# Differential attention, cross attention and merge as one program: moved norm and moved loads in a fused encoder layer

## What is computed

```
h = rmsnorm(x); proj = h @ w_in
o_a = gla_branch(...) * silu(z_a)
o_b = diff_attention(d_q, d_k, d_v) * silu(z_b)     # rmsnorm of each head's output
o_c = memory_cross_attention(c_q, mem) * silu(z_c)  # 256 memory tokens, 4 heads of 128
merged = sum_i sigmoid(gate_i) * (o_i @ w_branch_i)
y = rmsnorm(x + merged @ w_out)
```

## Time and profile before

| what | value |
|---|---|
| median of 3 runs | 3347.8 us (3347.14 to 3348.02) |
| span of the profiled execution | 3339.5 us |
| PE busy | 3254.0 us, 97% |
| DVE, ACT, POOL busy | 60%, 40%, 33% |
| diff ends, cross begins (PE) | about 2671 us |
| cross ends, merge begins (PE) | about 2778 us |

### The profile page before, as it was taken

One profiled execution on the slowest core, in us unless ns is written; L12 is line 12 of the kernel. 1 busy time (PEld: TensorE's weight loads), 2 busy tenths in 40 slices (PEclk: granted clock), 3 DMA queues, 4 the chain that ended last, 5 costly groups with the idle time before them and its releaser, 6 DMA issues. The chain is left out here.

```text
span 3339.5 us, 50988 instructions
## 1 busy us (share of the span) xinstructions
PE 3254.0 (97%) x19012; PEld 2544.6 (76%) x19012; DVE 2009.0 (60%) x4622; ACT 1331.0 (40%) x2171; POOL 1103.7 (33%) x511
## 2 busy tenths in 40 slices
PE   8999999999999999999999988999999898999998
PEld 6888888887888888888877865666666566888887
DVE  3322312226667666766667779888888567556654
ACT  3111111114334433444333336666766565223421
POOL 3322313244333333333333425555555442000000
PEclk9999999999999999999999989999999999999999
DMA  7545445465454544544459964122121268667562
GB/s 224 186 163 183 164 153 180 166 219 196 143 187 140 198 141 145 184 139 145 131 177 303 352 211 122 44 80 73 51 64 39 105 217 272 231 219 246 173 218 73
DMA packets 319014, 555.63 MB, mean 166 GB/s; under 512 B 35694, under 2 KB 115438, under 8 KB 318768
## 3 DMA queue, kind: packets, MB, share of 16 engines
q1 hardware_dynamic: 267296, 471.66, 43.4%
q10 hardware_dynamic: 51472, 80.71, 6.7%
HBM read 382.43 MB, written 169.82 MB: 165 GB/s over the span
## 5 line engine op out<-in xcount | busy, mean ns | idle before, releaser
L781 POOL TENSOR_TENSOR glaf_w_lo<-early_raw,glaf_w_hi 128x1024 fp32r<-128x1024 f32 x140 | 344.6, 2462 | 612.4 <-ACT glaf_w_hi L755 610.8
L810 PE MATMUL glaf_dense_acc<-h_hi,glaf_w_hi 128*128 128x512 f32 x1120 | 450.0, 402 | 0.5 <-ACT glaf_w_hi L755 0.5
L810 PE MATMUL glaf_dense_acc<-h_lo,glaf_w_hi 128*128 128x512 f32 x1120 | 438.4, 391 | 0.0
L810 PE MATMUL glaf_dense_acc<-h_hi,glaf_w_lo 128*128 128x512 f32 x1120 | 435.5, 390 | 0.0
L1814 DVE CUSTOM_DVE_ANT_0 front_p<-diff_s_ps,ahead_table 128x512 f32<-128x512 f32 x544 | 347.3, 687 | 70.7 <-PE diff_s_ps L1676 69.7
L555 POOL TENSOR_TENSOR proj_w_lo<-early_raw,proj_w_hi 128x1024 fp32r<-128x1024 f32 x84 | 202.8, 2414 | 477.3 <-DVE proj_w_hi L505 477.3
L1757 ACT ACTIVATE front_p<-front_p,diff_neg_max 128x2048 f32<-128x2048 f32 (+1 forms) x160 | 278.8, 1743 | 7.0 <-DVE diff_neg_max L1822 7.0
L1700 PE MATMUL diff_oT_ps<-diff_aT,diff_v 128*128 128x512 f32 x544 | 272.7, 602 | 4.8 <-ACT diff_aT L1751 4.8
L215 PE MATMUL proj_acc<-h_hi,proj_w_hi 128*128 128x512 f32 x672 | 262.9, 391 | 0.6 <-POOL proj_w_lo L555 0.6
L217 PE MATMUL proj_acc<-h_hi,proj_w_lo 128*128 128x512 f32 x672 | 261.6, 389 | 0.0
L216 PE MATMUL proj_acc<-h_lo,proj_w_hi 128*128 128x512 f32 x672 | 261.5, 389 | 0.0
(11 more groups left out here) (223 smaller groups left out, 7144.9 us busy)
## 6 DMA issues: line engine op xcount, KB each, us to landing
early_raw<-in_w_zg SPq DMA_DIRECT2D x180, 512.0 KB, 4.5
early_raw<-in_w_stream SPq DMA_DIRECT2D x80, 512.0 KB, 3.6
scratch_zg<-glaf_dense_out SPq DMA_DIRECT2D x140, 256.0 KB, 2.2
items_raw<-in_w_br SPq DMA_DIRECT2D x120, 256.0 KB, 3.0
merge_gate<-scratch_zg SPq DMA_DIRECT2D x120, 256.0 KB, 3.3
scratch_featT<-proj_out ACTq DMA_DIRECT2D x80, 256.0 KB, 2.4
items_br_hi<-scratch_item_hi SPq DMA_DIRECT2D x60, 256.0 KB, 5.9
items_br_lo<-scratch_item_lo SPq DMA_DIRECT2D x60, 256.0 KB, 6.6
```

The costliest lines, as they stand in the source:

```text
L781: pool.tensor_tensor(self.w_lo[:, s], self.raw[:, u % self.RAW], self.w_hi[:, s], ALU.subtract).then_inc(self.lo_split, 1)
L810: done = pe.matmul(self.acc[:, u % self.banks], a, x, start=i == 0, stop=i == self.PER - 1)
```

## The change

The three phases share one `Block`, so that no barrier stands between them; buffers that change hands are guarded by semaphore waits instead. diff's loops run to turn 82 on every engine (`OWN` = 83); the bodies of its turn loops become functions (`pe_turn`, `act_turn`, `dve_turn`, `pool_turn`), and cross calls them for turns 83 to 87 between its first tiles. On PE: scores 0, turn 83, scores 1, turn 84, scores 2, turn 85, scores 3, transposes 0, turn 86, scores 4. On ACT the evacuations of turn 84 alternate with the exponentials of tile 0; turn 85 precedes exponentials 1, turn 86 follows exponentials 4. On DVE turn 85 follows maximum 2, and turn 86 the evacuation of tile 0. On POOL turn 85 precedes the scaling of tile 1, and turn 87 that of tile 4.

Loads: memory 0 is asked for after turn 77 is mixed, q of chunks 0 and 1 after turn 78, z and memory 1 after turn 79. The stores of groups 18 and 19 are in cross's queue, behind the weight pieces and ahead of the item loads. At merge, weight pieces 4 to 6 come first, then the gates, both ahead of cross's last two chunks of stores; w_out and the gain stand between these two. The final clearing of semaphores follows the shared block. Some buffers are allocated in another order so that the overlaps fit. The preload of the Exp table in cross is gone.

```diff
@@ -74,6 +75,9 @@
                 used.clear()
                 self.nc.all_engine_barrier()
 
+        if shared is not None:
+            used.extend(self.allocated)
+            return shared
         self.ctx.callback(clear)
         return self.ctx.enter_context(self.nc.Block())
 
...
         LAST = TURNS + LAG + 1
+        OWN = LAST - 3
...
                             load_k(n)
             load_z(NG - 1)
-            sp.wait_ge(near_done, TURNS)
-            sp.wait_ge(far_done, TURNS)
-            front.load(sp)
-            for g in range(NG - 3, NG):
-                store(g)
-        @block.gpsimd
-        def _(pool):
-            pool.memset(ones[:, :], 1.0).then_inc(ones_ready, 1)
-
+
+            def combined(turns):
+                sp.wait_ge(near_done, turns)
+                sp.wait_ge(far_done, turns)
+
+            combined(TURNS - 2)
+            front.load_memory(sp, 0)
+            combined(TURNS - 1)
+            for c in range(2):
+                front.load_q(sp, c)
+            store(sp, NG - 3)
+            combined(TURNS)
+            for c in range(2):
+                front.load_z(sp, c)
+            front.load_memory(sp, 1)
+
...
             items.load_w(sp)
-            for semaphore, value in diff_stores:
+            diff.store(sp, diff.groups - 2)
+            diff.store(sp, diff.groups - 1)
+            for semaphore, value in diff.stores:
                 sp.wait_ge(semaphore, value)
             items.load(sp, 0, 2 * H)
             for c in range(2, NC):
                 sp.wait_ge(scores_done, TT * (c - 1))
                 front.load_q(sp, c)
                 if c >= 3:
-                    store(c - 3)
+                    store(sp, c - 3)
                     sp.wait_ge(gated, H * (c - 2))
                     front.load_z(sp, c - 1)
                 if c == 3:
                     sp.wait_ge(stored[0], 32 * H)
                     items.load(sp, 2 * H, 3 * H)
-            store(NC - 3)
+            store(sp, NC - 3)
             sp.wait_ge(gated, H * (NC - 2))
             front.load_z(sp, NC - 1)
-            store(NC - 2)
-            store(NC - 1)
 
...
@@ -1989,6 +2047,8 @@
                     pe.wait_ge(q_in[c % 2], 16 * (c // 2 + 1))
                 if n in (0, SEQS[0] // P):
                     pe.wait_ge(kT_in[sequence(n)], 16)
+                if n == 0:
+                    pe.wait_ge(diff.biased, diff.units_biased)
                 if n >= 2:
                     pe.wait_ge(p_ready, n - 1)
                 for h in range(H):
@@ -1997,6 +2057,8 @@
 
             def transposes(n):
                 pe.wait_ge(p_scaled, n + 1)
+                if n == 0:
+                    pe.wait_ge(diff.aT_ready, diff.units)
                 for k in range(MT):
                     if n:
                         pe.wait_ge((pT_dve, pT_act)[k], n)
@@ -2009,6 +2071,9 @@
                 pe.wait_ge(pT_dve, TT * (c + 1))
                 pe.wait_ge(pT_act, TT * (c + 1))
                 pe.wait_ge(v_in[sequence(c * TT)], 16)
+                if unit == 0:
+                    pe.wait_ge(diff.y_ready, diff.groups)
+                    pe.wait_ge(diff.outT_ready, diff.groups)
                 if unit >= 2:
                     pe.wait_ge(gated, unit - 1)
                 for k in range(MT):
@@ -2018,6 +2083,11 @@
             for n in range(N + BEHIND):
                 if n < N:
                     scores(n)
+                if n < LAG + 1:
+                    if n == LAG:
+                        transposes(0)
+                    diff.pe_turn(pe, CLOSE + n)
+                    continue
                 if 0 <= n - BEHIND < N:
                     values(n - BEHIND)
                 if 0 <= n - LAG < N:
@@ -2025,22 +2095,27 @@
 
         @block.scalar
         def _(act):
-            act.preload_act_table(ACT.Exp)
+            def exponential(n, h):
+                return act.activation(p[:, n % SLOTS, h], s_ps[:, n % 2, h], ACT.Exp, bias=neg_max[:, n % 2, h:h + 1], scale=SCALE,
+                                      accum_out=total[:, n % 2, h:h + 1])
 
             def exponentials(n):
                 act.wait_ge(max_steps, 2 * n + 2)
+                if n == 1:
+                    act.wait_ge(diff.values_done, diff.units)
                 if n >= 2:
                     act.wait_ge(inverted, n - 1)
                 if n >= SLOTS:
                     act.wait_ge(turned, 2 * (n - SLOTS) + 2)
                 for h in range(H):
-                    done = act.activation(p[:, n % SLOTS, h], s_ps[:, n % 2, h], ACT.Exp, bias=neg_max[:, n % 2, h:h + 1], scale=SCALE,
-                                          accum_out=total[:, n % 2, h:h + 1])
+                    done = exponential(n, h)
                 done.then_inc(p_ready, 1)
 
             def evacuate(n):
                 c, t = divmod(n, TT)
                 act.wait_ge(turned, 2 * n + 2)
+                if n == 0:
+                    act.wait_ge(diff.turned, diff.units)
                 if c >= 2 and t == 0:
                     act.wait_ge(values_done, H * (c - 1))
                 act.activation(pT[:, c % 2, 1, :, t * P:(t + 1) * P], t_ps[:, 1].rearrange("p (h t) -> p h t", h=H), ACT.Copy).then_inc(pT_act, 1)
@@ -2052,9 +2127,18 @@
                 act.wait_ge(gated, unit + 1)
                 act.activation(out_hi[:, c % 2, h], prod[:, unit % 2], ACT.Copy).then_inc(out_high, 1)
 
-            for n in range(N + BEHIND):
+            diff.act_turn(act, CLOSE)
+            act.wait_ge(max_steps, 2)
+            for h in range(H):
+                diff.evacuate(act, CLOSE + 1, h)
+                done = exponential(0, h)
+            done.then_inc(p_ready, 1)
+            diff.act_turn(act, CLOSE + 2)
+            for n in range(1, N + BEHIND):
                 if n < N:
                     exponentials(n)
+                if n == LAG + 1:
+                    diff.act_turn(act, CLOSE + 3)
                 if 0 <= n - LAG < N:
                     evacuate(n - LAG)
...
@@ -2101,6 +2187,8 @@
             for n in range(N + BEHIND + 1):
                 if n < N:
                     maximum(n)
+                if n == LAG - 1:
+                    diff.dve_turn(dve, CLOSE + 2)
                 if 0 <= n - 1 < N:
                     invert(n - 1)
                 if 0 <= n - BEHIND - 1 < N:
@@ -2109,16 +2197,23 @@
                     product(n - BEHIND)
                 if 0 <= n - LAG < N:
                     evacuate(n - LAG)
+                if n == LAG:
+                    diff.dve_turn(dve, CLOSE + 3)
                 if 0 <= n - N // 2 < items.SPLIT:
                     items.low(dve, n - N // 2)
 
         @block.gpsimd
         def _(pool):
+            diff.pool_turn(pool, CLOSE)
             for n in range(N):
+                if n == 1:
+                    diff.pool_turn(pool, CLOSE + 2)
+                if n == LAG + 1:
+                    diff.pool_turn(pool, CLOSE + 4)
                 pool.wait_ge(inverted, n + 1)
                 pool.tensor_tensor(p[:, n % SLOTS], p[:, n % SLOTS], inverse[:, n % 2].unsqueeze(2).broadcast_to([P, H, N_MEM]), ALU.mult).then_inc(p_scaled, 1)
 
-    return [(stored[b], 32 * H * ((NC + 1 - b) // 2)) for b in range(2)]
+        return CrossEnd(store, NC, scores_done, N, turned, 2 * N, values_done, gated, N, p_ready, [(stored[b], 32 * H * ((NC + 1 - b) // 2)) for b in range(2)])
 
...
@@ -2246,14 +2342,18 @@
                 sp.wait_ge(normed, n + 1)
                 sp.dma_start(rows(y, n * P, P), x[:, n % XS]).then_inc(y_out[n % XS], 16)
 
+            for u in range(AHEAD):
+                load_w(u + RAW)
+            sp.wait_ge(cross.scores_done, cross.tiles)
             for u in range(GS):
                 load_gate(u)
+            cross.store(sp, cross.chunks - 2)
+            sp.wait_ge(cross.turned, cross.turns)
             for kt in range(XS):
                 load_wo(kt)
             sp.dma_start(gain[:, :], final_gain).then_inc(gain_in, 16)
-            for u in range(AHEAD):
-                load_w(u + RAW)
-            for semaphore, value in cross_stores:
+            cross.store(sp, cross.chunks - 1)
+            for semaphore, value in cross.stores:
                 sp.wait_ge(semaphore, value)
             for c in range(NC):
...
@@ -2309,6 +2409,8 @@
 
             def wo_split(kt):
                 act.wait_ge(wo_in[kt % XS], 16 * (kt // XS + 1))
+                if kt == 0:
+                    act.wait_ge(cross.values_done, cross.units)
                 act.activation(wo_hi[:, kt], x[:, kt % XS], ACT.Copy).then_inc(wo_high, 1)
 
...
@@ -2344,6 +2446,8 @@
             def branch(u):
                 c, d, b = place(u)
                 s = u % RING
+                if u == 0:
+                    pe.wait_ge(cross.p_ready, cross.tiles)
                 pe.wait_ge(lo_split, u + 1)
                 if u >= RING:
                     pe.wait_ge(combined, u - RING + 1)
@@ -2356,6 +2460,7 @@
 
             def outputs(c):
                 if c == 0:
```

(11 more changed lines are left out.)

275 lines of the change are left out of this document (159 added, 116 removed).

## The result

The changed kernel takes 3349.5 us (median of 21 runs, 3346.4 to 3352.2), the kernel before, beside it, 3345.8 (median of 21, 3341.9 to 3348.0). The ratio is 1.0014, 95% interval 1.0007 to 1.0020: slower, by 3.7 us between the medians, by 4.7 by the ratio (2.3 to 6.7). 3339.6 was predicted, with a range of 3332 to 3345.5. The direction was wrong, the range too low.

The account below looks back on a forecast made before the run. TensorE, busy to the end, was taken to bound the kernel. Seam one's +1.65 and seam two's -9.8 sum to -8.15: span 3331.35, with 8.3 around it 3339.6 us; range 3332 to 3345.5.

Parts of the forecast that it names:

- The base: Span of the profiled execution, 3339.5 us, with 8.3 added at the end to reach the median of three runs, 3347.8.
- S0: Scores of cross tile 0, first in seam one's new order, taking the place of diff turn 83: start at 2646.4.
- S4: Scores of cross tile 4, seam one: start at 2669.85, 14.2 us sooner than 2684.10.
- the norm's chain: Last group's norm in seam one: VectorE done 2667.65, GpSimd's diagonal 2668.8, TensorE waits 0.8 us ahead of the spread.
- SyncE's queue: Seam one: q 2, behind group 19's store and 16 item loads, lands at 2696.7; a 14 us wait takes back the gain.
- S8: Scores of cross tile 8: start at 2696.8 instead of 2682.7; from there on +1.65 us with the low clock.
- rival (a): Both seams pay in full, with q 2 there by 2683: -24.0 us, 3323.8; chance 0.10.
- The low clock: After the wait at tile 8 its scores run at the lower clock: 1.74 us lost, as at tile 16.
- rival (c): Slower: after 14 us of idling before S8 the clock stays low; with 31 us more, 3354.6; chance 0.07.
- Seam two's gap: Cross to merge: merge follows the last values at once, 4.95 us and 0.15 of overlap, 5.1 won.
- Merge's first units: Start of merge: 1.5 us won from the cold start, 2.2 from unit 4's piece, 1.0 of 1.9 from other waits.
- Rival (b): Seam two pays only the seam; merge's 4.1 us of waits stay or come back elsewhere: -4.95, 3342.8; chance 0.15.

Follow-up runs that it names:

- e4: Changed kernel with q 2 loaded once tile 3's scores are done, ahead of group 19's store and the item loads: 3330.1 us, ratio 0.9959.
- e8: Changed kernel with stat allocated behind wo_lo, which begins at byte 117376 again: 3342.8 us, ratio 0.9993.
- e1: Changed kernel with stat 64 bytes wide instead of 32, so wo_lo begins at 117440: 3347.9 us, ratio 1.0006.
- e5: Changed kernel with SyncE's wait for cross's last stores moved to the first load that overwrites an item buffer: 3348.0 us, ratio 1.0010.
- e12: Kernel before with stat ahead of wo_hi (32 bytes off) and 96 bytes of padding ahead of wo_lo: 3346.4 us, ratio 1.0012.
- e2: Kernel before with stat (32 bytes) allocated ahead of wo_lo, nothing else: 3351.1 us, ratio 1.0022.
- e11: e9 plus q 4 loaded after tile 11's scores, and w_out's splits spread over merge units 4 to 18, loads two units later: 3318.5 us, ratio 0.9922.
- e9: Changed kernel with the edits of e4, e5 and e8, plus w_out's loads four units and ScalarE's splits two units later: 3325.2 us, ratio 0.9943.

## Why the prediction was wrong, point by point

**The base.** "8.3 around" the span was read wrongly: it is 1.8 (3352.2 against 3350.4), and the other 6.5 us were the distance of a quick execution to the median. In the sum this does no harm, since it only leads back to the median of three runs, 3347.8. But that median lay 2.0 above the one of 21 runs, 3345.8; from there the same sum gives 3337.7, so 2 us of the 3339.6 were luck.

**S0, S4, the norm's chain: right.** S0 was forecast at 2646.4 and S4 at 2669.85; less the 5.1 us by which the changed profile reaches the mark later, they came at 2646.4 and 2669.5, with the forecast wait of 0.8 at the spread.

**SyncE's queue: right.** The low half of group 19 was forecast for 2677.3 and items for 2680.3; less the drift its store was issued at 2678.5 and the first item at 2680.9; q 2 was issued at 2689.3, where the prediction had 2689.7. q 2 let S8 start 17.1 us after the first item, inside the 14.7 to 18.0, and S8 began at 2697.9 instead of 2696.8. That seam one would be won and given back at S8 is shown by the 13.62 us row and by e4. What rival (a) had over the forecast, 14 us at S8 and the low clock, is what e4 gave when the queue was turned round (13.8 and 3.1).

**The low clock: the term was too small.** 1.74 us was taken from tile 16, after 3.15 us of idling. After 13.62 us, S8 to S9 took 7.43 instead of 4.32 (2696.89 to 2701.21 before, S8 in the earlier trace rows): 3.1 us, since not only the scores but the values behind them ran slowly. Other versions with the same wait lost 3.1 (e8), 2.7 (e1) and 1.9 (e5). So the step's price was 3.1 where 1.74 stood; it and 1.1 us by which S8 came later make the first column's miss, less 0.3 from seam two. Nor is tile 16's price a fixed one: 0.1, 1.8 or 3.1 us after nearly the same idling (e12, before, e2). The clock recovered each time; rival (c)'s staying low didn't happen.

**Seam two's gap: right.** 5.1 us forecast; the values run into merge without idling, and the step from S9 to merge's first matmul is 5.4 us shorter (+4.16 against before at S9, -1.25 at merge, both from the mark).

**Merge's first units: this step failed.** 4.7 us were to be won (cold start, unit 4's piece, 1.0 of the others) and 0.85 were lost. Unit 4's wait did go. The sentence that failed is "q, z and stores go out ahead of them or wait for nobody": it looked at the pieces loaded early and not at the next one. The last stores now go out behind gates, w_out and the gain, while merge already runs; SyncE's wait for them, which had cost nothing, became 9.9 us, and weight piece 7 stood behind it. GpSimd has the same wait of its own ahead of w_out's low halves, which reuse memory that the stores still read. The two together are the step: SyncE's put off alone (e5) gave 0.3 us of the stage back, and with GpSimd's work spread as well (e11) 4.25 of the 5.55 missed. The prediction's "late next is VectorE", beside GpSimd, was the right engine; that the wait for the stores would bunch GpSimd's work, and so VectorE's stretching, was not seen. Rival (b) had this engine, but priced it as waits that stay, not as a new one with a clock drop behind it.

**The outputs: missing from the sum.** "Some buffers are allocated in another order so that the overlaps fit" stood in the description of the change and got neither a price nor a rival. It cost 6.2 us, and decides the sign of the result: without it (e8) the changed kernel isn't told apart from the one before. Even then the forecast gain of 8 didn't come; the other two misses took it.

The three misses, 2.2 + 5.55 + 6.2, are 13.95 us: forecast -8.15, came +5.8 by the marks of the two profiles. By medians it is +3.7 (interval 2.3 to 6.7).

## What to carry to other kernels

When barriers between phases fall, follow each queue past the seam up to its first wait for a landing, and ask what stands behind it: here SyncE's order gave back all 14 us of one seam, its wait together with GpSimd's took some 4 of the other, and two lines in the right place (q 2 ahead of 4 MiB of items) were worth 19 us, where the change as it stood had won less than 1 on its two seams together. An engine that was held up should not find a pile of work when it is let go, if it shares something with the engine that paces. And a diff that reorders allocations changes a kernel even where no instruction does: compare the start addresses of what TensorE streams and holds.

## What the hardware showed that was not expected

- In the 960 output matmuls, a streamed operand (128x512, f32 storage) that starts 32 or 64 bytes past a multiple of 128 in its partition raised the pace from 226.8 ns to 231.2 to 233.3, averaged over blocks of 192, with no wait anywhere in the trace. 32 bytes of padding decide 6 us of 3345. In the branch matmuls, where streamed and held operand both start 96 bytes past, the pace is 226.8.
- After 13.3 to 13.6 us of TensorE idling in cross, the granted clock stayed at its lower level for 3.7 to 6.1 us of the work behind it, and one tile's work (8 scores, 4 values, 8 transposes) took 6.2 to 7.5 us instead of 4.32, in four versions of the same wait. After 3.0 to 3.6 us of idling at tile 16 the clock fell in some executions and not in others (e4, e9, e12), with the same code.
- The same code reached the same instruction (the mark) at 2641.1 to 2647.3 us in five executions. What comes behind the mark up to merge still differed by up to 3 us between them, with tile 16's clock; merge's first 24 units agreed within 0.4 us.
